# Heads of a hybrid encoder: two token blocks as one seven-product group, tokens normalised once a layer, head outputs kept in DRAM

## The reference

```
x = x + 0.5 * swiglu(rmsnorm(x, norm_ffn1), ...)
h = rmsnorm(x, norm_mix)
rq, rk, rv, rg, dq, dk, dv, g_ret, g_dil = split(h @ w_in)
y_ret = retention(rq, rk, rv, rg) @ w_ret_o          # 4 heads, rope on q and k, silu gate
y_dil = dilated_attention(dq, dk, dv, norms, bias) @ w_dil_o   # 3 groups x 4 heads
merged = sigmoid(g_ret + b) * y_ret + sigmoid(g_dil + b) * y_dil
x = x + merged @ w_out
x = x + 0.5 * swiglu(rmsnorm(x, norm_ffn2), ...)
```

## Time and profile before

| | |
|---|---|
| median of three runs | 2623.45 us (2622.6 to 2624.01) |
| span of the profiled execution | 2621.4 us |
| PE busy | 2614.9 us, 100% |
| DVE, ACT, POOL busy | 68%, 42%, 2% |
| granted TensorE clock | 1.00 in all stretches |

### The profile page before, as it was taken

How to read it: one execution, slowest core, us unless ns; L and a number is a source line. 1 busy time by engine, 2 the same in 40 slices (tenths; PEclk the granted TensorE clock), 3 DMA queues, 4 the chain that set the end, 5 groups by cost and what they waited for, 6 DMA issues and landing times.

```text
span 2621.4 us, 38953 instructions
## 1 busy us (share of the span) xinstructions
PE 2614.9 (100%) x14961; PEld 2318.4 (88%) x14961; DVE 1775.0 (68%) x2394; ACT 1094.2 (42%) x1567; POOL 63.3 (2%) x79
## 2 busy tenths in 40 slices
PE   9999999999999999999999999999999999999999
PEld 7999988888888888999989999888888888889998
DVE  8877765574665468777788777664755645697776
ACT  5433444454543234333443344444544522343432
POOL 1111000000000000000000000000000000000000
PEclk9999999999999999999999999999999999999999
DMA  5433243233224333333223232432322343333231
GB/s 186 150 117 112 81 136 94 81 98 92 86 63 145 99 105 116 107 98 103 97 81 121 96 97 72 154 92 65 117 81 80 96 122 93 121 111 99 96 105 56
DMA packets 225756, 269.96 MB, mean 103 GB/s; under 512 B 14036, under 2 KB 182401, under 8 KB 225101
## 3 DMA queue, kind: packets, MB, share of 16 engines
q1 hardware_dynamic: 220488, 259.09, 31.4%
q0 software_dynamic: 4512, 5.04, 0.7%
q10 hardware_dynamic: 646, 4.31, 0.4%
HBM read 259.75 MB, written 13.28 MB: 104 GB/s over the span
## 4 chain that ended last, share of the span: by engine, by line
PE 99%; DVE 1%; DMA 0%; issue 0%; ACT 0%; SPq 0%; DVEq 0%; ACTq 0%
PE proj L557 25%; PE proj L559 25%; PE proj L558 25%; PE acc L558 7%; PE acc L557 7%; PE acc L559 7%; PE acc L880 1%; PE acc L819 0%; PE acc L839 0%; PE acc L802 0%; PE acc L803 0%; PE acc L829 0%; PE acc L804 0%; PE acc L828 0%; DMA raw<-in_w_in 0%
## 5 line engine op out<-in xcount | busy, mean ns | idle before, releaser
L557 PE MATMUL proj<-h_hi,ring_hi 128*128 128x256 f32 (+1 forms) x1632 | 548.8, 336 | 0.7 <-DVE h_lo L1607 0.7
L559 PE MATMUL proj<-h_hi,ring_lo 128*128 128x256 f32 (+1 forms) x1632 | 544.1, 333 | 0.0
L558 PE MATMUL proj<-h_lo,ring_hi 128*128 128x256 f32 (+1 forms) x1632 | 543.7, 333 | 0.0
L557 PE MATMUL proj<-y_hi,ring_hi 128*128 128x256 f32 (+1 forms) x1504 | 463.3, 308 | 0.0
L559 PE MATMUL proj<-y_hi,ring_lo 128*128 128x256 f32 (+1 forms) x1504 | 463.0, 308 | 0.0
L558 PE MATMUL proj<-y_lo,ring_hi 128*128 128x256 f32 (+1 forms) x1504 | 463.0, 308 | 0.0
L1143 ACT ACTIVATE ring_hi<-raw 128x1024 fp32r<-128x1024 f32 (+1 forms) x175 | 209.9, 1203 | 360.4 <-PE acc L559 194.6
L557 PEld LDWEIGHTS proj<-h_hi,ring_hi 128*128 128x128 f32 x1632 | 310.1, 190 | 32.6 <-DVE h_lo L1607 1.7
L559 PEld LDWEIGHTS proj<-h_hi,ring_lo 128*128 128x128 f32 x1632 | 309.9, 190 | 30.5
L558 PEld LDWEIGHTS proj<-h_lo,ring_hi 128*128 128x128 f32 x1632 | 310.2, 190 | 28.7
L559 PEld LDWEIGHTS proj<-y_hi,ring_lo 128*128 128x128 f32 x1504 | 287.3, 191 | 13.7
(11 more groups left out here) (277 smaller groups left out, 3663.7 us busy)
## 6 DMA issues: line engine op xcount, KB each, us to landing
raw<-in_ffn_gate SPq DMA_DIRECT2D x88, 512.0 KB, 3.6
raw<-in_ffn_up SPq DMA_DIRECT2D x88, 512.0 KB, 4.0
raw<-in_w_in SPq DMA_DIRECT2D x136, 256.0 KB, 3.6
raw<-in_w_in SPq DMA_DIRECT2D x60, 512.0 KB, 4.9
raw<-in_ffn_down SPq DMA_DIRECT2D x56, 512.0 KB, 4.4
work<-in_ffn_down SPq DMA_DIRECT2D x32, 512.0 KB, 5.7
raw<-in_w_out SPq DMA_DIRECT2D x16, 512.0 KB, 4.2
raw<-in_w_ret_o SPq DMA_DIRECT2D x12, 512.0 KB, 3.8
```

The source lines that it names most:

```text
L557: pe.matmul(o, s_hi, m_hi, start=start, stop=False, skip_group_check=onto)
L558: pe.matmul(o, s_hi, m_lo, start=False, stop=False, skip_group_check=onto)
L559: return pe.matmul(o, s_lo, m_hi, start=False, stop=stop, skip_group_check=onto)
```

## The change

Each pair of 512-column token-major blocks (tokens 512 x k 1024 times 1024 columns) is now one seven-product group over halves of tokens, of k and of columns. Units 3 and 4 are the two k-halves of rg, and units 5 to 11 the products M1, M5, M3, M6, M7, M2, M4, each two token tiles x 4 k; a head has twelve units.

```
-HEAD_TILES = [2, 4, 4, 2, 4, 4, 4, 4]
+HEAD_TILES = [2, 4, 4, 2, 2] + [2] * PROD
+M1, M5, M3, M6, M7, M2, M4 = range(5, 12)
+HEAD_PRODUCTS = {M1: (A11, 0, False), M5: (S1, 2, False), M3: (S4, 2, True), M6: (N2, 0, True), M7: (S3, 0, True),
+                 M2: (A12, 2, False), M4: (A22, 0, True)}
```

The weight blocks B11, B12, B22, B21 land in `raw`, now four slots. POOL makes T1 = B12 - B11, T2 = T1 - B22, T3 = T2 + B11 and T4 = T2 + B21 in place:

```
+                with pool.Fori(0, RET_HEADS) as n:
...
+                    pool.wait_ge(block_landed[B12], 64 * (H + 1))
+                    pool.tensor_tensor(second, second, first, ALU.subtract).then_inc(t_made, 1)
...
+                    pool.tensor_tensor(second, second, third, ALU.subtract).then_inc(t_made, 1)
+                    pool.wait_ge(t_made, 4 * H + 2)
+                    pool.tensor_tensor(first, second, first, ALU.add).then_inc(t_made, 1)
...
+                    pool.tensor_tensor(second, second, third, ALU.add).then_inc(t_made, 1)
```

Head outputs are written to `y_spill` in DRAM and come back for the merge into `y_lo`; ACT and DVE split them there. The merge's first units are reordered, its gates read the banks straight into the sigmoid, and the six `qk_turn` steps of the last head run there:

```
+                sp.wait_ge(ret_sum, H + 1)
+                sp.wait_ge(ret_spilled, 16 * H)
+                for i in range(RET_HEADS - 1):
+                    y_reload(i, slice(2 * i, 2 * i + 2))
...
+                def y_his(i):
+                    act.wait_ge(y_in[max(0, i - 2)], (48 if i < 3 else 16) * (l + 1))
```

More of the change, by code:

```diff
@@ L423, in ffn, with done_lo @@
                 down_rows(l, f, GROUPS - 1, place=raw[:, 1, :])
[L425 to L439, removed]
+            def done_lo(index):
+                sp.wait_ge(weights_lo, index + LO_CREDIT)
@@ L483, in _ @@
                 sp.dma_start(perm_f, c_perm).then_inc(perm_in, 16)
[L484 to L491, removed]
+                head_units(l, 0, False)
@@ new lines, in bank_copy, with squares @@
+            def bank_copy(tile, k, b, place, counter):
+                bank = HEAD_PRODUCTS[k][1] + b
+                done(tile + HEAD_TILE[k] + b)
+                act.activation(place, four(PB[bank]), ACT.Copy).then_inc(counter, 1)
+            def squares(H, at, x, b):
+                c = x * NB + b
+                if not isinstance(H, int) or SUMMED * H + at >= 3:
+                    act.wait_ge(qk_summed, SUMMED * H + at - 2)
+                act.activation(sq_out[at % 3], qk_tile[x][:, b * P:(b + 1) * P], ACT.Square,
+                               accum_out=qk_ss[:, c:c + 1]).then_inc(qk_summed, 1)
@@ L1447, in heads @@
-                split_qkv(at(4), H, 2)
+                    values(0)
+                    values(1)
+                    dil_exps(H - 1, 2)
+                    values(2)
+                    values(3)
+                    dil_exps(H - 1, 3)
+                    hi(4)
+                    dil_factors(H - 1)
+                else:
+                    hi(2)
+                    norm_copy(first)
+                    swap_halves(H, 1, T + 1)
+                    hi(3)
+                    operand(0)
+                    operand(1)
+                    hi(4)
+                    for b in range(NB):
+                        values(b)
+                    operand(2)
@@ new lines, in heads @@
+                act.wait_ge(ret_v_ready, 4 * H + 4)
+                act.activation(ret_v_hi[:, :, :], ret_v, ACT.Copy).then_inc(ret_v_hi_ready, 1)
+                if prev:
+                    act.wait_ge(q0_copied, 4 * H + 4)
+                    for b in range(NB):
+                        squares(H, b, 0, b)
+                hi(5)
+                if not prev:
+                    operand(3)
+                    operand(4)
+                for e in (0, 1):
+                    if prev:
+                        done(T + HEAD_TILE[4] + e)
+                        act.wait_ge(ret_y, 4 * H)
+                        act.activation(silu[:, e, :], PB[2 + e][:, :], ACT.Silu).then_inc(silu_ready, 1)
+                    else:
+                        act.wait_ge(rg_scaled, 2 * l + e + 1)
+                        act.activation(silu[:, e, :], silu[:, e, :], ACT.Silu).then_inc(silu_ready, 1)
@@ L1488, in heads @@
[L1488 to L1500 removed]
+                hi(11)
@@ L1533, in merge @@
+                split(at(9), 1536)
+                split(at(10), 1536)
+                split(at(11))
+                merged_hi(M0 + 2, 0)
+                for p in range(2, KT // 2):
+                    at = lambda k: unit(l, MERGE_BASE + 11 + 5 * (p - 2) + k)
+                    M = M0 + 2 * p
+                    split(at(1))
+                    merged_hi(M - 1, 1)
+                    gate(M, 0, PB[2])
+                    gate(M, 1, PB[3])
                     split(at(2), 1536)
-                    gate(M0 + 2 * p, 2 * p, 1, 0)
```

1225 lines of the change are left out of this document (741 added, 484 removed).

## The result

The changed kernel takes 2683.59 us (2682.64 to 2685.76, three runs) against 2623.45: the ratio is 1.0231 with a 95% interval of 1.0213 to 1.025. It is slower by 60 us, where the forecast was 8 us slower and the range ended at 2664.

A forecast was written before the change was run, and what follows sets the result against it. TensorE was taken to bound the kernel, a queue of matmuls without a hole. Net changes of -18.2 (loop heads), +10.9 (first heads) and +15 (merge) gave +7.7, span 2629.1 us, time 2631; range 2598 to 2664.

The forecast's parts named there:

- The matmuls that go: All heads: 24 fewer matmuls a head at 0.2267 us each, 5.44 us a head, 43.5 us for eight heads.
- Place 1: M1 in six loop heads: TensorE waits 2.4 us, each head changes by -3.0 us, six by -18.2.
- Place 3: Start of the merge, two layers: waits at the scores and dil_move, 7.5 us each, +15 in all.
- place 2: First head of each layer: waits of 6.0, 3.0 and 1.9 us, sum 10.9; two heads change by +10.9.
- the third one: First heads: M3's split stands behind four operands and two rotary splits and is 1.9 us late.
- rival (a): POOL sums and two-operand DVE splits take turns: loop heads +2.5 us, first heads +6.5, sum 28, time 2659; chance 0.31.
- none is late by itself: POOL's four sums a head: first ready some 16 us before its split is wanted, the others 5 to 12 us.
- A wait that the change adds costs its full length: Whole kernel: an added TensorE wait costs its full length, since no wait is there to take it up.
- rival (d): Clock falls in new holes: four long holes each lose 3.2 us at half speed, +13, time 2644; chance 0.06.

The follow-up runs named there:

- x11: Changed kernel with M1's chain shortened, merge and first heads reordered, sums on DVE, further order changes and a merge weight load issued earlier: 2587.47 us.
- x2: Changed kernel with POOL's four sums a head left out, all waits kept: 2652.7 us.
- x6: Changed kernel with each of POOL's sums cut into four instructions of 128x512: 2672.72 us.
- x10: Changed kernel with M1's chain shortened, merge and first heads reordered and further order changes, but POOL still making the four sums: 2625.84 us.
- x1: Changed kernel with matmuls of ones filling most of each long TensorE wait, nothing else changed: 2665.18 us.
- x13: As x12, with eight matmuls of ones in front of M1 in each of the six loop heads: 2602.62 us.
- x12: As x11, but with the changed kernel's order in the loop heads, DVE still making the sums: 2605.84 us.
- x4: Changed kernel with the merge reordered, hi-parts of the reloaded outputs behind the q and k copies, fourth sigmoid gate behind the exponentials: 2666.47 us.

## Why the prediction was wrong

The matmuls that go (43.5 us) were right; x11 shows the same size from the other side.

Place 1 was right in mechanism and nearly in size: 2.4 us said, 2.06 or 2.07 in all six. Place 3 too: 5 us said at the scores, 5.9 and 4.9 found; 2.5 at dil_move, 3.3 found; the reload on which ACT waits came at E+16 and not E+15.5. In place 2 the gate unit was said to wait 6.0 us and waited 7.5 and 7.3. Of the rest 0.9 us lies in the first split, which started inside POOL's first sum and took 2.10 us and not 1.22, and most of what is left in the normalising operations, with a pitch of 0.66 us and not 0.61; without POOL's sums, in x2, the wait is 6.7. M5 was said to wait 3.0 and waited 2.6.

The step that failed in place 2 is the third one. "Then M3's split stands behind four operands and two rotary splits (...) and is 1.9 us late": TensorE stood 7.1 and 8.7 us already for the two rotary splits, which the first retention score wants, and 0.6 more for M3's split. The work in the list was right; the durations were not, since three operands took 12.2 us instead of 3.5 while POOL summed. That is rival (a). The prediction treated it as another case with a chance of 0.31 beside the forecast, and wrote "none is late by itself" of the sums: none was, but their neighbours were. The trace of before could not show it, as the earlier trace rows have the split start after POOL's end (in one of the eight cases it starts 0.13 us before it, and takes its usual 2.29). x2, x6 and x10 show it: 31 us without the sums, 11 us when the same work is cut into quarters, and 31 us again in an order with hardly another hole. That the rival's sum of 28 us is near this is luck: it had 6.5 us for a first head, where POOL's sums made holes of 7.1 and 8.7, and 2.5 for a loop head, where they made 0.5. That is 18.8 us of holes in all, and most of the rest of the 31 is slower matmuls, which the rival did not have. The Trainium skill ("SBUF — State Buffer", Who interferes with whom) has the rule, and this trace agrees with it: 12.21 us and 0.55 us, above. Of POOL's sum, 5.2 us was taken; it takes 4.60 alone and up to 5.38. The Trainium skill's 4.5 ("GPSIMD Engine Reference", 3.1 Elementwise) is nearer, with 4.6 in this trace.

The larger failure is what a hole costs. "A wait that the change adds costs its full length": it costs more. Behind 14 of the 16 holes of 2 us or more the clock is at its lower level for 3 to 6 us, and some 30 of the 60 us are this. The prediction had it as rival (d), with a chance of 0.06, for four long holes at 3.2 us each: 13 us. Two things made it too small. There are 16 holes of 2 us or more and not four (three in each first head, six at M1, two in each merge; eight of about half a us besides), and holes of 2 us, which the rival didn't count, were followed by a low clock in five of six heads. x1 shows that idling is the cause, since ones in the same place take 27 of the 33 us away; x13 agrees, by 3.2 us, in a kernel with hardly another hole. What decides whether one 2 us hole is followed by it is not settled: x12 has it in two of six heads whose lists are the same, x4 in all six.

The largest error of all is in the form. The three causes were set as cases beside each other, with a chance each, and the range was drawn round one. They act together: 2631 with the sums of the orders, 18 more by POOL's holes, 33 by slower matmuls (nearly all the clock) gives 2682. That the orders' part fits so well is partly luck: its waits were said to be 51.2 us (6 x 2.4 + 2 x 10.9 + 15) and are 50.4 (69.2 - 18.8), with M1, M5 and M3 shorter than said, the gate unit and the merge longer.

## What to carry to other kernels

Where TensorE is busy without a hole, price a new hole at its length and then ask of the clock: here a hole of 2 us was followed by a low clock in 24 cases of 42, and a hole can be filled with matmuls of ones into a free bank to see how much that is. Work given to POOL is not free to DVE: what counts is which two-operand DVE instructions fall into its time. And causes that do not exclude each other belong into one sum, not into separate cases.

## What the runs showed of the hardware

- A DVE operation with two SBUF inputs that starts while POOL runs a two-input sum ends after POOL, by nearly its own length: a split of 128x1024 (1.22 us alone) that started at 382.92 took 2.10 and ended at 385.02, 1.07 us after POOL's 379.34 + 4.61 = 383.95; the one of 128x512 above (0.69 alone) ended 0.55 us after POOL.
- It is not only operations with two large inputs: a TENSOR_SCALAR of 128x2 (L2216, one SBUF input) took 3.73 us at 498.00 and ended at 501.73, as POOL's sum did (497.09 + 4.61 = 501.70), while two reductions of 128x256 just before it, inside the same sum, took 0.74 us together.
- A DVE operation of two inputs of which one is in PSUM (`proj`) was not held: inside a two-input sum of POOL it took 0.69 us, as one of 128x512 does elsewhere.

```profile
562.45 1.30 POOL L665 TENSOR_TENSOR work<-work 128x512 f32<-128x512 f32 x1
```

```profile
562.56 0.69 DVE L2333 TENSOR_TENSOR xs<-xs,proj 128x512 f32<-128x512 f32 x1 [0.88 <-PE proj L678]
```

- A 128x2048 sum on POOL takes 4.60 us, less than four times the 1.29 of the 128x512 one.
- Where the clock falls behind a hole of 2 us differs from hole to hole, from its end to 1.3 us behind it in the five cases of the changed kernel. Behind the hole that ends at 519.12 TensorE worked at full speed to about 520.4; behind the one that ends at 721.77 it was slow at once:

```profile
721.80:724.80 3.00, 3.00 (x7) 2.41 (x8) 1.70 (x2) 1.71 (x1) 0.00 (x0) 0.51 0.00 0
```
